# Turning attention probabilities in 32x32 blocks on VectorE, with DMA to place them

## What is computed

```python
def second_block(x, ...):
    h = rmsnorm(x, g_norm)
    a_u, a_v, a_gate, q, k, v, b_gate, gate_logits = split(h @ w_in)
    y_a = chunked_spatial_gating(gelu(a_u), gelu(a_v), w_s, b_s, g_v) * silu(a_gate)
    y_b = dilated_attention(q, k, v) * silu(b_gate)
    merged = g_a * (y_a @ w_proj_a) + g_b * (y_b @ w_proj_b)   # g_a, g_b: sigmoid of gate_logits
    return rmsnorm(x + merged @ w_out, g_final)
# dilated_attention, per head: s = q k^T / 8 - slope * distance, masked, causal
#   p = exp(s - max) / sum ; o = p v   (three windows of 128, 512, 2048 with dilations 1, 4, 16, weighted by their sums)
```

## Time and profile before

| | us |
|---|---|
| median of 3 runs | 1377.52 (1376.96 to 1377.62) |
| the profiled execution | 1377.27 |
| its span | 1375.5 |
| PE busy | 1359.8 (99% of the span) |
| PE weight loads busy | 1105.1 (80%) |
| DVE busy | 805.3 (59%) |
| ACT busy | 594.9 (43%) |
| POOL busy | 71.2 (5%) |

### The profile page before, as it was taken

One profiled execution on the slowest core, in us unless ns is written; L12 is line 12 of the kernel. 1 busy time (PEld: TensorE's weight loads), 2 busy tenths in 40 slices (PEclk: granted clock), 3 DMA queues, 4 the chain that ended last, 5 costly groups with the idle time before them and its releaser, 6 DMA issues.

```text
span 1375.5 us, 17410 instructions
## 1 busy us (share of the span) xinstructions
PE 1359.8 (99%) x6399; PEld 1105.1 (80%) x6399; DVE 805.3 (59%) x1258; ACT 594.9 (43%) x1007; POOL 71.2 (5%) x60
## 2 busy tenths in 40 slices
PE   7999999999999999999999999999999999999998
PEld 6787777778888888888888888877787787788886
DVE  7768888785675553354445554745654565455544
ACT  7435555554464441223433345733443343342233
POOL 1000000102002000000023200000000000000000
PEclk9999999999999999999999999999999999999999
DMA  5333333233333333323333332332322223222332
GB/s 160 92 92 77 78 75 95 66 118 107 93 92 101 97 92 107 105 80 92 106 92 91 95 106 91 96 95 67 92 82 87 75 79 94 78 80 84 100 109 75
DMA packets 224103, 127.01 MB, mean 92 GB/s; under 512 B 21234, under 2 KB 214851, under 8 KB 224034
## 3 DMA queue, kind: packets, MB, share of 16 engines
q1 hardware_dynamic: 222418, 123.47, 31.1%
q10 hardware_dynamic: 1616, 2.62, 0.6%
HBM read 123.98 MB, written 2.10 MB: 92 GB/s over the span
## 4 chain that ended last, share of the span: by engine, by line
PE 96%; DVE 2%; ACT 1%; issue 1%; ACTq 0%; DVEq 0%
PE lin L642 26%; PE lin L646 25%; PE lin L645 25%; PE ob L1060 1%; PE sc L749 1%; PE sc L725 1%; PE sc L1016 1%; PE sc L1020 1%; PE sc L1019 1%; PE tr L738 1%; PE ob L762 1%; PE tr L1019 1%; PE lin L1019 1%; PE lin L1020 1%; PE tr L1020 1%
## 5 line engine op out<-in xcount | busy, mean ns | idle before, releaser
L1661 DVE TENSOR_TENSOR wl<-raw,wh 128x1024 fp32r<-128x1024 f32 (+2 forms) x235 | 288.0, 1233 | 83.6 <-ACT wh L1181 79.1
L1181 ACT ACTIVATE wh<-raw 128x1024 fp32r<-128x1024 f32 (+2 forms) x235 | 238.6, 1024 | 136.6 <-DMA raw<-in_w_mlp_dram 42.8
L642 PE MATMUL lin<-uh,wh 128*128 128x512 f32 x624 | 251.3, 403 | 0.7 <-DVE ul L1714 0.4
L646 PE MATMUL lin<-uh,wl 128*128 128x512 f32 x624 | 243.3, 390 | 0.0
L645 PE MATMUL lin<-ul,wh 128*128 128x512 f32 x624 | 243.1, 390 | 0.0
L642 PE MATMUL lin<-vh,wh 128*128 128x512 f32 x512 | 206.4, 403 | 0.0
L646 PE MATMUL lin<-vh,wl 128*128 128x512 f32 x512 | 200.1, 391 | 0.0
L645 PE MATMUL lin<-vl,wh 128*128 128x512 f32 x512 | 199.5, 390 | 0.0
L642 PEld LDWEIGHTS lin<-uh,wh 128*128 128x128 f32 x624 | 117.2, 188 | 28.7 <-issue 5.2
L645 PEld LDWEIGHTS lin<-ul,wh 128*128 128x128 f32 x624 | 117.3, 188 | 26.0 <-issue 3.1
L646 PEld LDWEIGHTS lin<-uh,wl 128*128 128x128 f32 x624 | 117.1, 188 | 24.7
(11 more groups left out here) (557 smaller groups left out, 2036.6 us busy)
## 6 DMA issues: line engine op xcount, KB each, us to landing
raw<-in_w_in_dram SPq DMA_DIRECT2D x100, 512.0 KB, 3.8
raw<-in_w_mlp_dram SPq DMA_DIRECT2D x64, 512.0 KB, 4.0
raw<-in_w_out_dram SPq DMA_DIRECT2D x16, 512.0 KB, 3.7
raw<-in_w_xkv_dram SPq DMA_DIRECT2D x8, 512.0 KB, 3.7
raw<-in_w_proj_b_dram SPq DMA_DIRECT2D x8, 512.0 KB, 3.7
raw<-in_w_proj_a_dram SPq DMA_DIRECT2D x8, 512.0 KB, 3.6
xtok<-in_x_dram ACTq DMA_DIRECT2D x4, 512.0 KB, 5.0
raw<-in_w_mla_out_dram SPq DMA_DIRECT2D x4, 512.0 KB, 3.5
```

The costliest lines, as they stand in the source:

```text
L642: ins = pe.matmul(o, wh[:, slot, at], xh_, start=start, stop=False)
L646: return pe.matmul(o, wl[:, slot, at], xh_, start=False, stop=stop)
L1181: act.activation(wh[:, c.slot(4), 0:size], raw[:, c.slot(2), 0:size], ACT.Copy).then_inc(hi_made, 1)
L1661: dve.tensor_tensor(wl[:, c.slot(4), 0:size], raw[:, c.slot(2), 0:size], wh[:, c.slot(4), 0:size].bitcast(F32), ALU.subtract).then_inc(lo_ ...
```

## The change

PE's turns of the probabilities and both sets of copies out of the banks go, in the 16 heads of the phase `pairs` only. DVE's own transpose turns each 32x32 block in place within its four groups of 32 partitions and writes them to a buffer `blocks` (five instructions a head, 1280 columns in all; `turn_blocks`). SP then issues sixteen transfers a head (`place_blocks`), each of 32 partitions by 1280 bytes (40 KB), which move the blocks from partition group q to partition group k of `first_turned` or `second_turned`. These two buffers lie over memory that was free or holds queries and keys. `weigh_pair` reads them with columns in runs of 32, and waits for all 32 transfers of the pair; it moves from k = 3 to k = 7 of job 6. SP's transfers stand between the loads of chunks: the first head's behind the load of chunk c+7, the second head's behind c+8. PE's waits at the end of a pair move to the scores of the next, and after the last pair to the end of the phase. On DVE the second head's mask moves ahead of the first head's scaling, the gelu's two steps go to both sides of `turn_blocks`, and the second head's maxima come ahead of `lower(c + 6)`; on ACT the second head's exponentials go ahead of the gate's tanh.

The diff, cut to its core:

```diff
+            def place_blocks(g, p):
+                sp.wait_ge(blocks_turned, 2 * g + p + 1)
+                sp.wait_ge(second_scores_ready, 3 * g + 3)
+                for k in range(4):
+                    for q in range(4):
+                        sp.dma_start(BLOCK_TURNED[p][32 * k:32 * k + 32, q, :, :].rearrange("p b x -> p (b x)"),
+                                     blocks[32 * q:32 * q + 32, k, :, :].rearrange("p b x -> p (b x)"))\
+                            .then_inc(blocks_landed, 16)
             for i in range(PAIRS):
                 c = phase("pairs")[0] + 7 * i
                 for m, first in enumerate((3, 4, 0, 2, 6, 7, 8)):
                     load(c + m, w_in2, first * D + P * i, DT, P)
+                    if i and m < 2:
+                        place_blocks(i - 1, m)
...
             def weigh_pair(g):
-                pe.wait_ge(turned_act, HEADS + 2 * g + 2)
-                pe.wait_ge(turned_dve, 2 * g + 2)
+                pe.wait_ge(blocks_landed, 2 * LANDED * (g + 1))
                 for kb in range(QT):
                     for p in range(2):
                         rows, at = slice(64 * p, 64 * p + 64), kb * P + 64 * p
-                        ins = pe.matmul(ob[rows, kb * P:S], gb[:, g, at:at + 64], WEIGHTS[p][kb], start=kb == 0,
-                                        stop=kb == QT - 1)
+                        ins = pe.matmul(ob[rows, kb * P:S], gb[:, g, at:at + 64],
+                                        BLOCK_TURNED[p][:, :, BLOCKS_AT[kb], :].rearrange("p a b x -> p b a x"),
+                                        start=kb == 0, stop=kb == QT - 1)
...
                 def score():
                     evacuated(pe, j)
                     evacuated(pe, j + 1)
                     pe.wait_ge(av_taken, 2 * QT)
+                    pe.wait_ge(mix_read, g + 1)
+                    wait(pe, yb_made, g)
                     scores_of_two(n0)
...
                 job(c + 2, j + 2, DT, vh, vl, between={4: score})
-                job(c + 3, j + 3, DT, vh, vl, between={6: lambda: turn_rows(n0, TURNED[0], (0, 1, 2))})
-                job(c + 4, j + 4, DT, vh, vl, between={0: lambda: turn_rows(n0, TURNED[0], (3,))})
-                job(c + 5, j + 5, DT, vh, vl, between={
-                    0: turn_mixing, 4: lambda: turn_rows(n1, TURNED[1], (0, 1, 2)),
-                    6: lambda: turn_rows(n1, TURNED[1], (3,))})
-                job(c + 6, j + 6, DT, vh, vl, between={0: mix, 3: lambda: weigh_pair(g)})
-                pe.wait_ge(mix_read, g + 2)
-                pe.wait_ge(yb_made, g + 1)
+                job(c + 3, j + 3, DT, vh, vl)
+                job(c + 4, j + 4, DT, vh, vl)
+                job(c + 5, j + 5, DT, vh, vl, between={0: turn_mixing})
+                job(c + 6, j + 6, DT, vh, vl, between={0: mix, 7: lambda: weigh_pair(g)})
...
+            pe.wait_ge(mix_read, PAIRS + 1)
+            pe.wait_ge(yb_made, PAIRS)
...
# ACT, in a pair
                 split(c + 6)
-                copy_first_keys(n0, 0)
+                exps(n1)
                 evacuated(act, j + 2)
                 act.activation(ta[:], read(j + 3)[:], ACT.Tanh, scale=0.5).then_inc(silu_tanh, 1)
-                exps(n1)
                 split(c + 7)
...
-                copy_first_keys(n1, 1)
                 split(c + 8)
...
# DVE
+            def turn_blocks(n):
+                k = n.static - HEADS
+                wait(dve, probs_scaled, n.times(4, 4))
+                wait(dve, blocks_landed, LANDED * k)
+                for q in range(QT):
+                    m = min(q + 1, 3)
+                    dve.transpose(blocks[:, :, q:q + 3 * m - 2:3, :],
+                                  logit[:, LOFF[q]:LOFF[q] + P * m].rearrange("p (b k x) -> p k b x", b=m, k=4))
+                dve.transpose(blocks[:, :, 7, :], logit[:, 1280 - P:1280].rearrange("p (k x) -> p k x", k=4))\
+                    .then_inc(blocks_turned, 1)
...
                 maxima(n0, banks=FIRST, scored=g + HEADS)
+                mask(n1, 2 * i + 1)
                 scale_probs(n0)
+                bend(j + 2, g.times(1, 1))
+                turn_blocks(n0)
                 gelu(j + 2, g.times(1, 1), tb[:])
-                mask(n1, 2 * i + 1)
+                dve.wait_ge(blocks_turned, 2 * i + 1)
+                maxima(n1, second_scores_ready, scored=g)
                 lower(c + 6)
-                copy_other_keys(n0, 0)
-                maxima(n1, second_scores_ready, scored=g)
                 dve.wait_ge(silu_tanh, g.times(2, 1))
...
                 scale_probs(n1)
+                turn_blocks(n1)
...
-                copy_other_keys(n1, 1)
                 lower(c + 8)
```

More of the change, by code:

```diff
@@ L234, in build @@
         logit = sb("logit", [P, 1280])
+        st = ExitStack()
+        first_turned = sb("first_turned", [P, 4, 10, 32], stack=st)
+        st.close()
         pt = sb("pt", [P, 896])
@@ L240, in build @@
         qt = sb("qt", [P, S])
+        st = ExitStack()
+        second_turned = sb("second_turned", [P, 4, 10, 32], stack=st)
+        st.close()
         kt = sb("kt", [P, S])
         vtok = sb("vtok", [P, QT, P])
-        ta, tb, tc, td, te = (sb(n, [P, S]) for n in ("ta", "tb", "tc", "td", "te"))
+        td, ta, tb, tc, te = (sb(n, [P, S]) for n in ("td", "ta", "tb", "tc", "te"))
         bias = sb("bias", [P, S])
@@ L277, in build @@
         st.close()
+        st = ExitStack()
+        st.enter_context(nc.sbuf_tensor("low_ya", [P, PAIRS * S - P], F32))
+        blocks = sb("blocks", [P, 4, 10, 32], stack=st)
+        st.close()
         ya = sb("ya", [P, PAIRS, S])
@@ L303, in build @@
         AV_WORK = ((ta, tb), (te, bias))
-        mem_landed, vecs_landed, taps_landed, consts_landed, pos_landed = (
-            sem(n + "_landed") for n in ("mem", "vecs", "taps", "consts", "pos"))
+        mem_landed, vecs_landed, taps_landed, consts_landed, blocks_landed = (
+            sem(n + "_landed") for n in ("mem", "vecs", "taps", "consts", "blocks"))
         x_landed = [sem(f"x{q}_landed") for q in range(QT)]
@@ L331, in build @@
         probs_scaled, turned_ready = sem("probs_scaled"), sem("turned_ready")
-        turned_act, turned_dve = sem("turned_copied_scalar"), sem("turned_copied_vector")
+        turned_act, blocks_turned = sem("turned_copied_scalar"), sem("blocks_turned")
         scores_ready, logits_made, probs_made = sem("scores_ready"), sem("logits_made"), sem("probs_made")
@@ L430, in build @@
         H_COPIED = {f: k + 1 for k, f in enumerate(H_ORDER)}
-        TURNED = ([(tr[0], 0), (tr[1], 0), (ob, 0), (tr[1], 384)], [(sc[0], 0), (sc[1], 0), (sc[2], 0), (sc[2], 256)])
-        WEIGHTS = ([qt[:, 0:512], kt[:, 0:384], pts[:, 0:256], kt[:, 384:512]],
-                   [pt[:, 0:512], pt[:, 512:896], pts[:, 256:512], pts[:, 512:640]])
+        TURNED = [(sc[0], 0), (sc[1], 0), (sc[2], 0), (sc[2], 256)]
+        BLOCK_TURNED = (first_turned, second_turned)
+        BLOCKS_AT = [slice(0, 4), slice(4, 7), slice(8, 10), slice(7, 8)]
+        LANDED = 16 * 16
         FIRST_WEIGHTS = ([pa[:, 0:512], pa[:, 512:896], pa[:, 896:1152], pa[:, 1152:1280]],
@@ L488, in _ @@
                     sp.dma_start(qt[64:128, :].bitcast(I32), a["positions"][0].partition_broadcast(64))\
-                        .then_inc(pos_landed, 16)
+                        .then_inc(consts_landed, 16)
                 load(c + m, w_in, 2 * CONV + P * m, DT, P)
@@ L556, in _ @@
                         sp.dma_start(bsb, biases).then_inc(gating_landed, 16)
-            stream("proj_b", a["w_proj_b_2"][0], 0, DT, P)
+            c, _ = phase("proj_b")
+            for m in range(DT):
+                load(c + m, a["w_proj_b_2"][0], P * m, DT, P)
+                if m < 2:
+                    place_blocks(PAIRS - 1, m)
             stream("proj_a", a["w_proj_a_2"][0], 0, DT, P)
@@ L863, in turns @@
             def turns(n, *rows):
-                turn_rows(Idx(n), TURNED[1], rows)
+                turn_rows(Idx(n), TURNED, rows)
             for u in range(HEADS // 2):
@@ L1074, in turn_mixing @@
                     pe.wait_ge(ws_masked, g + 1)
-                    pe.wait_ge(turned_act, HEADS + 2 * g + 1)
+                    wait(pe, logits_made, n1.times(4, 1))
                     pe.transpose(tr[0][:, 0:P], ws, ident[:]).then_inc(wst_ready, 1)
@@ L1079, in mix @@
                     pe.wait_ge(atok_placed, g + 1)
-                    pe.wait_ge(turned_dve, 2 * g + 1)
                     pe.wait_ge(wst_placed, g + 1)
@@ L1234, in o_split @@
                 act.activation(oh[:, at, :], ob[:], ACT.Copy).then_inc(o_high, 1)
-            def copy_first_keys(n, p):
-                wait(act, turned_ready, n.times(1, 1))
-                act.activation(WEIGHTS[p][0], TURNED[p][0][0][:], ACT.Copy).then_inc(turned_act, 1)
             act.wait_ge(start_made, 2)
@@ L1771, in rope_arguments @@
                 r = slice(64, 128)
-                dve.wait_ge(consts_landed, 16)
-                dve.wait_ge(pos_landed, 16)
```

(4 more changed lines are left out.)

## The result

The changed kernel takes 1425.78 us (1425.09 to 1426.11, 4 runs) beside 1377.24 us for the kernel before: a ratio of 1.0353, with a 95% interval of 1.0337 to 1.0368. It is 48.5 us slower, where 16.9 us less were forecast, and lies outside the range. The profiled execution has a span of 1424.0 us.

A forecast was written before the change was run, and what follows sets the result against it. TensorE, with 96% of the chain, was taken to bound the kernel. Turns saved 17.6 us less 0.7 at the end, 16.9 us off 1377.27: 1360.4, as median of runs 1360.6; range 1358.5 to 1377.5 us.

The forecast's parts named there:

- TensorE's turns are on the path: Removing turns around the squares in each pair of heads saves 2.2 us a pair, 17.6 us over eight pairs.
- rival F: More is gained than the turns (products spaced closer, no loss at the end): below 1359 us; chance 0.03.
- The weighing's operand at no cost: TensorE's weighing reads columns in runs of 32 and still takes 2.30 us; nothing added.
- Rival D: The weighing is slower with the hops: at the double, 8 x 2.3 = 18.4 us, 1379.0 us; chance 0.04.
- VectorE's turns, 1.7 us: Five added transpose instructions over 1280 columns a head on VectorE take 1.7 us.
- Rival B: VectorE turns at half rate, transfers land 1.9 us late: 16 us lost, 1376.6 us, no change; chance 0.07.
- The sixteen transfers, 0.38 us apart: SP issues a head's transfers 0.38 us apart, the last 5.7 us after the first.
- the margin of 0.8 us: The second head's transfers land at 949.1, 0.8 us before TensorE asks for the weighing at 949.9: no stall.
- rival C: SP's issue is the bound: at 0.53 us each, landed 3.1 us late a pair, 25 us, 1385.7 us; chance 0.13.
- The landing, 2.1 us: A transfer lands 2.1 us after issue; transfers overlap, so it is paid once: 7.8 us a head.
- The chain: Attention steps of a pair, from first maxima at 924.56 to second head's transfers landed at 949.1, in time.
- Other waits: Chunk loads behind transfers hidden; job 6's bank freed some two microseconds early; end of last pair costs 0.7 us once.

The follow-up runs named there:

- the kernel with four transfers: Against the changed kernel: same bytes in four transfers a head (128 partitions by 1280 bytes) instead of sixteen, no move between partition groups; 1358.43 us, ratio 0.9864.
- the nine others of that kernel: Unprofiled executions with twelve transfers a head instead of the changed kernel's sixteen, same bytes, no move between partition groups; 1376.76 us over 10 runs, ratio 0.9997.

## Why the prediction was wrong

- **What bounds the kernel, and that TensorE's turns are on the path**: right. Where the transfers are in time the gain is 18.75 us (1377.18 to 1358.43), with 17.6 less 0.7 forecast, 16.9. So with the transfers in time the kernel stands 2.2 us under the 1360.6 of my sum; rival F had half of the reason, products spaced closer. A pair fell from 46.36 to 44.00 us, 2.36 and not 2.2. My term counted the distance around the turns and the one product behind it, against 0.23; in the kernel with four transfers 38 products in a row start 0.227 apart. With 0.227 for the undisturbed spacing the two distances at each of the four groups of turns come to 2.23 us. Most of the other 0.13 lies further behind: in the earlier trace rows the spacing from 932.45 to 933.37 (four products) is 0.230, and behind the second group several start 0.23 to 0.236 apart.
- **The weighing's operand at no cost**: right, 2.30 us in both forms. Rival D falls.
- **VectorE's turns, 1.7 us**: right, 1.66 us. Rival B falls. The Trainium skill's one element per cycle and lane ("Vector Engine (DVE) Microarchitecture Reference", section 3.8) agrees with the trace: 384 columns take 0.54 us and 128 take 0.27, about 1.05 ns a column, the rate that the prediction read from the earlier trace rows for other instructions (1.04).
- **The sixteen transfers, 0.38 us apart**: this is the step that failed, and with it the margin of 0.8 us. The measured distance is 0.63 to 0.67 us, and the last transfer landed 5.1 us after TensorE's question in the second pair. Of three distances (0.38, 0.41, 0.53) I chose the cheapest, by the form of what it carried (long rows), and the form turned out not to matter. Two things made it too small. First, 0.38 is the distance behind the first issue of a row, the short one: in the earlier trace rows the second takes 0.43 us and not 0.34, so with 0.04 between two a third would have come 0.47 behind it. At 0.47 an issue the formula of rival C already has the transfers 1.3 us late (937.1 + 30 x 0.47 = 951.2). The rows could have told me that. Second, both ends in SBUF, which took it from 0.47 to 0.63; that no row showed.
- **The landing, 2.1 us, and the overlap of transfers**: right, 1.9 us. The Trainium skill's rule against many small transfers ("DMA: Bandwidth & Descriptors", section Rules for kernel authors), which I weighed and set aside, gave the right sign. On spreading DMAs over several engines the Trainium skill says, in the section Issuing engines are not separate DMA queues of the same page, that it saves only the sequencer's time to initiate, usually small relative to the DMA itself. In this case that time was not small: in the second pair the issues of the second head took 9.7 of the 11.6 us from its first issue (949.71) to its last landing (961.3), and spreading them over two queues gave 67 us.
- **The chain**: its form was right. Rival C's formula, 937.1 + 30 x issue, gives 956.3 at 0.64 us, which is 31.7 us behind the first maxima (924.56); measured were 31.98 us (929.36 to 961.34). It put the wait at 6.4 us a pair, 51 us in all; TensorE waited 40.0 + 8.4 = 48.4 us. 8.4 us of them lie at job 6, since VectorE's late turn holds up the gate step that frees its bank; I had that order in view and gave it two microseconds to spare, which holds only if the first head's transfers are in time.
- **The chances**: C had 0.13. With 0.53 among three distances and nothing like the new transfers among them, the upper end deserved more. And C's own price was too low: at 0.64 us it says 1360.6 + 51 = 1412, and 1425.8 was measured. What it lacks is what comes behind each wait, for the most part the slow clock. The sum comes out with it: the profiled execution with four transfers took 1358.1 us; the waits of 48.4 us and the 19.2 us by which the same matmuls were busy longer make 1425.7, and 1425.75 was measured. No rival had this term: I let a wait cost its own length.
- **Other waits**: the loads behind the transfers did no harm where the transfers were in time. With sixteen issues the loads of c+9 started at 960.02 and no job waited for a chunk. Behind the last pair 0.7 us were forecast, and in the kernel with four transfers TensorE waits 0.6 us there for VectorE.

## What to carry to other kernels

Count the issues on each queue in a chain that has an end time, and price one issue by a row with the same two memories at its ends; if there is none, take the dearest row (0.53 us here, which was still too low). Take the price from the second issue of a row or a later one, since the first is shorter. Then ask for the point at which the chain becomes late (here 0.43 us an issue), and treat a price that no row bounds as a coin toss around that point. A wait on TensorE costs more than its length when the granted clock falls to its lower level in it; and a chain that is limited by issuing can be split over two queues (1358.4 us here) or go through DRAM in fewer transfers (1358.9).

## What the runs showed of the hardware

- In a row of issues on SP's queue, one transfer with both ends in SBUF took 0.60 to 0.64 us for 4 to 160 KB, 16 to 128 partitions and rows of 128 to 2048 bytes; from DRAM to SBUF it took 0.43 to 0.46 us (16 to 160 KB), and from SBUF to DRAM 0.56 us (256 KB). SBUF to SBUF, 40 KB, it took 0.64 us on ScalarE's queue and 0.50 on GpSimd's.
- The first issue of a row was shorter than those behind it: 0.51 against 0.59 us within SBUF, 0.31 to 0.35 against 0.42 out of DRAM. A load of 512 KB took 0.37 us to issue alone and 0.58 right behind transfers within SBUF; the runs don't show why.
- In waits of 4.8 to 5.8 us TensorE's granted clock fell to 0.50, and it was back at 1.00 only 2.7 to 6.0 us after work began again; in the profiled execution with waits of 1.3 to 2.4 us it stayed at 1.00, while the nine others of that kernel had a mean of 0.994 to 0.998.
- 640 KB out to DRAM and back, placed, took 9.2 us from the first issue to the last landing of the first head in the second pair (928.62 to 937.82), against 12.0 us (935.86 to 947.84) for the same placement in sixteen transfers within SBUF.
